# Eight chunks of the modulation matrix worked on by TensorE inside the first attention instead of by VectorE beside the output projection

## The reference

```
cond = silu(c)
mod = cond @ w_ada + b_ada            # 2048 x 12288: shift1, scale1, gate1, shift2, scale2, gate2
h = rms(x, norm1_w) * (1 + scale1) + shift1
u, q, k, v = split(h @ w_in)
y_ssm = s5_mixer(u);  y_ssm = y_ssm * sigmoid(y_ssm @ w_glu)
y_att = dilated_attention(q, k, v)    # 8 heads of 128
x = x + gate1 * (concat(y_ssm, y_att) @ w_out)
h2 = rms(x, norm2_w) * (1 + scale2) + shift2
x = x + gate2 * swiglu_ffn(h2)
```

## Time and profile before

| | |
|---|---|
| three runs | 3303.84, 3310.92 and 3312.99 us, median 3310.92 |
| the profiled execution | 3305.19 us; its span 3303.4 us |
| TensorE busy | 3132.1 us, 95% of the span |
| VectorE busy | 1927.0 us, 58% |
| ScalarE busy | 1210.0 us, 37% |
| DMA | 630.47 MB, mean 191 GB/s |
| first attention's units | from 424.8 to 473.6 us of the span |
| first matmul of `glu`, of `w_out` | 480.70 us, 506.81 us |
| last matmul of `w_out` | about 616.5 us |

### The profile page before, as it was taken

The page is one execution under the profiler, slowest core; times in us unless marked ns, Lnnn a source line. Parts: engine busy times, 40 slices in busy tenths (PEclk is TensorE's granted clock), DMA queues, the critical chain, the costliest instruction groups (busy, mean ns, idle before and its releaser), DMA issues.

```text
span 3303.4 us, 57521 instructions
## 1 busy us (share of the span) xinstructions
PE 3132.1 (95%) x25282; PEld 3072.8 (93%) x25282; DVE 1927.0 (58%) x1816; ACT 1210.0 (37%) x1058; POOL 201.6 (6%) x194
## 2 busy tenths in 40 slices
PE   3399978899999999999999999999999999999999
PEld 2399858799999999999999999999899999999999
DVE  7999768776444444745445544564556554555454
ACT  2254433333333333433333333343334333333333
POOL 3344130000000000000000000000030000000000
PEclk6699969899999999999999999999999999999999
DMA  9776608678555555555555555567635555555554
GB/s 336 250 260 241 237 31 289 217 259 283 179 183 190 183 186 190 181 176 170 175 178 171 173 178 178 169 190 135 124 127 179 182 188 186 184 190 180 189 183 136
DMA packets 328703, 630.47 MB, mean 191 GB/s; under 512 B 22453, under 2 KB 24009, under 8 KB 328281
## 3 DMA queue, kind: packets, MB, share of 16 engines
q1 hardware_dynamic: 317512, 624.79, 57.8%
q10 hardware_dynamic: 11040, 3.51, 0.5%
HBM read 626.16 MB, written 2.10 MB: 190 GB/s over the span
## 4 chain that ended last, share of the span: by engine, by line
PE 81%; DVE 3%; issue 1%; ACT 1%; DVEq 0%; ACTq 0%
PE ps L545 23%; PE ps L546 23%; PE ps L547 23%; PE ps L1861 2%; PE ps L1863 2%; PE ps L1862 2%; PE ps L1898 1%; PE ps L1899 1%; PE ps L1900 1%; DVE w_lo L412 1%; DVE accb L426 0%; ACT w_hi L407 0%; PE ps L1802 0%; PE ps L1776 0%; PE ps L1812 0%
## 5 line engine op out<-in xcount | busy, mean ns | idle before, releaser
L412 DVE TENSOR_TENSOR w_lo<-raw,w_hi 128x2048 fp32r<-128x2048 f32 x496 | 1141.0, 2301 | 1229.5 <-ACT w_hi L407 1229.3
L407 ACT ACTIVATE w_hi<-raw 128x2048 fp32r<-128x2048 f32 x496 | 949.8, 1915 | 1777.9 <-PE ps L547 1550.9
L545 PE MATMUL ps<-act_hi,w_hi 128*128 128x256 f32 (+1 forms) x4288 | 1221.9, 285 | 46.0 <-DVE w_lo L412 23.1
L546 PE MATMUL ps<-act_lo,w_hi 128*128 128x256 f32 (+1 forms) x4288 | 1219.0, 284 | 0.0
L547 PE MATMUL ps<-act_hi,w_lo 128*128 128x256 f32 (+1 forms) x4288 | 1217.3, 284 | 0.0
L545 PEld LDWEIGHTS ps<-act_hi,w_hi 128*128 128x128 f32 x4288 | 814.1, 190 | 49.4 <-issue 29.4
L545 PE MATMUL ps<-hid_hi,w_hi 128*128 128x256 f32 (+1 forms) x2880 | 814.4, 283 | 7.1 <-DVE w_lo L412 7.1
L546 PEld LDWEIGHTS ps<-act_lo,w_hi 128*128 128x128 f32 x4288 | 813.8, 190 | 0.0
L547 PEld LDWEIGHTS ps<-act_hi,w_lo 128*128 128x128 f32 x4288 | 813.4, 190 | 0.0
L547 PE MATMUL ps<-hid_hi,w_lo 128*128 128x256 f32 (+1 forms) x2880 | 812.4, 282 | 0.0
L546 PE MATMUL ps<-hid_lo,w_hi 128*128 128x256 f32 (+1 forms) x2816 | 794.5, 282 | 0.0
(11 more groups left out here) (328 smaller groups left out, 2050.1 us busy)
## 6 DMA issues: line engine op xcount, KB each, us to landing
raw<-in_w_ada SPq DMA_DIRECT2D x96, 1024.0 KB, 5.1
raw<-in_ffn_w_gate SPq DMA_DIRECT2D x88, 1024.0 KB, 5.0
raw<-in_ffn_w_up SPq DMA_DIRECT2D x88, 1024.0 KB, 5.0
raw<-in_ffn_w_down SPq DMA_DIRECT2D x88, 1024.0 KB, 5.1
raw<-in_w_in SPq DMA_DIRECT2D x64, 1024.0 KB, 6.3
raw<-in_w_ffn_gate SPq DMA_DIRECT2D x44, 1024.0 KB, 5.0
raw<-in_w_ffn_up SPq DMA_DIRECT2D x44, 1024.0 KB, 5.1
raw<-in_w_ffn_down SPq DMA_DIRECT2D x44, 1024.0 KB, 5.1
```

What stands on the lines that cost most here:

```text
L407: act.activation(w_hi[b][:, :, :], raw[j % RING][:, :, :], ACT.Copy).then_inc(hi_ready, 1)
L412: dve.tensor_tensor(w_lo[b][:, :, :], raw[j % RING][:, :, :], w_hi[b][:, :, :].bitcast(F32), ALU.subtract).then_inc(lo_ready, 1)
L545: pe.matmul(o, whi, hi[:, k, cols], start=(k == 0 and not (shared and m % 2)), stop=False)
L546: pe.matmul(o, whi, lo[:, k, cols], start=False, stop=False)
```

## The change

Eight of the 16 V chunks leave `w_out`, whose pass is now `VSS` four times (8 V and 16 S chunks in all). They form a new phase `mid` of kind `P` between `w_in` and `glu`. TensorE multiplies them itself, out of `raw`, without VectorE: for each of 4 row tiles and 4 column tiles one matmul with the weights as stationary operand and one column of `cond` as moving operand, accumulated in PSUM bank 5. `beside(s_)` of the attention now does half a chunk, eight matmuls, in each of the steps 0 to 15. VectorE adds the bias at the end of the block. The ring's head at the end of `w_in` is now four `mid` chunks; the other four and the head of `glu` are issued during the attention.

```diff
-    add("w_out", 2, 2, 4, "VS" * 8)
+    add("mid", 1, 0, 4, "P" * 8)
...
+    add("w_out", 2, 2, 4, "VSS" * 4)
...
+            if name == "mid":
+                return lambda it, j: w_ada(j % 4, SCALE2 * P + (j // 4) * GROUP)
...
-            return {"S": (lo_ready, n), "V": (acc_step, CK * n)}[p.order[j]]
+            return {"S": (lo_ready, n), "V": (acc_step, CK * n), "P": (mid_done, n)}[p.order[j]]
...
-                stream(sp, "glu", rest=False)
+                stream(sp, "mid", rest=False)
...
+        def mid_pe(pe, s_):
+            p = byname["mid"]
+            for e in range(MID // 8 * s_, MID // 8 * (s_ + 1)):
+                j, half = divmod(e, 2)
+                if j >= MID:
+                    continue
+                if half == 0:
+                    landed(pe, p, 0, j)
+                for t in (2 * half, 2 * half + 1):
+                    for m in range(4):
+                        c = 4 * (j // 4) + m
+                        mm = pe.matmul(ps[:, 5, c:c + 1], raw[j % RING][:, t, P * m:P * m + P], cond[:, CK * (j % 4) + t:CK * (j % 4) + t + 1],
+                                       start=(e == 0 and t == 0 and m == 0), stop=(j == MID - 1 and t == CK - 1 and m == 3), skip_group_check=True)
+                if half:
+                    mm.then_inc(mid_done, 1)
...
+                stream(sp, "mid", head=False)
+                stream(sp, "glu", rest=False)
...
                 units_dve(dve, 0)
+                dve.wait_ge(mid_done, MID)
+                dve.tensor_tensor(gain[:, 0:MID], ps[:, 5, 0:MID], bada[:, SCALE2:SCALE2 + MID], ALU.add)
...
-                units_pe(pe, 0, nothing)
+                units_pe(pe, 0, lambda s_: mid_pe(pe, s_))
...
-                    dve.wait_ge(mod_sum, 20)
-                    link(dve, "dve", dve.tensor_tensor(gain[:, :], ps[:, 1, 0:16], bada[:, SCALE2:SCALE2 + 16], ALU.add))
+                    dve.wait_ge(mod_sum, 18)
+                    link(dve, "dve", dve.tensor_tensor(gain[:, MID:16], ps[:, 1, 0:16 - MID], bada[:, SCALE2 + MID:SCALE2 + 16], ALU.add))
...
-                for g in range(4):
+                for g in range(2):
```

More of the change, by code:

```diff
@@ L28 @@
 QUADS = KT // 4
+MID = 8
 SEQ = 256
@@ L100, in __init__ @@
         self.body = len(order)
-        self.per = {k: order.count(k) for k in "SV"}
+        self.per = {k: order.count(k) for k in "SVP"}
         self.n0 = tally["n"]
-        self.before = {k: tally[k] for k in "SV"}
+        self.before = {k: tally[k] for k in "SVP"}
         self.g0 = tally["g"]
         tally["n"] += iters * self.body
-        for k in "SV":
+        for k in "SVP":
             tally[k] += iters * self.per[k]
@@ L119, in plan @@
 def plan():
-    tally = {"n": 0, "g": 0, "S": 0, "V": 0}
+    tally = {"n": 0, "g": 0, "S": 0, "V": 0, "P": 0}
     ph = []
@@ L312, in build @@
         wf_split, wf_in = sem("wf_split"), sem("wf_in")
+        mid_done = sem("mid_done")
         tile_done, tile_free = sem("tile_done"), sem("tile_free")
@@ L337, in source @@
                 w = rows(a[name][0], 0, D)
-                first = GATE1 if name == "w_in" else SCALE2
-                return lambda it, j, v=None: w_ada(v % 4, first * P + (it * 2 + v // 4) * GROUP) if v is not None else w[:, CK * (j % 4):CK * (j % 4) + CK, bass.ds((j // 4) * GROUP + it * (2 * GROUP), GROUP)]
+                first, per = (GATE1 * P, 2) if name == "w_in" else (SCALE2 * P + (MID // 4) * GROUP, 1)
+                return lambda it, j, v=None: w_ada(v % 4, first + (it * per + v // 4) * GROUP) if v is not None else w[:, CK * (j % 4):CK * (j % 4) + CK, bass.ds((j // 4) * GROUP + it * (2 * GROUP), GROUP)]
             ffn, what = name.split(".")
@@ L837, in gate2_dve @@
         def gate2_dve(dve):
-            dve.wait_ge(mod_sum, 24)
+            dve.wait_ge(mod_sum, 22)
             dve.tensor_tensor(mod[:, GATE2:GATE2 + 16], ps[:, 4, 0:16], bada[:, GATE2:GATE2 + 16], ALU.add).then_inc(mod_read, 1)
```

## The result

The changed kernel takes 3350.65 us (median of 4 runs, 3349.97 to 3351.61) against 3308.26 us before (4 runs). The ratio is 1.0134, with a 95% interval of 1.0122 to 1.0146: 42 us slower.

What follows compares the result with a forecast made beforehand. The prediction took TensorE, busy for 95% of the span, to bound the kernel. Its terms, 4.7 + 52.8 + 0.2 - 3.9 = +53.8 us on a base of 3308, gave 3361 us, with a range of 3320 to 3372.

Steps and rivals of the forecast that it cites:

- Which stage pays, and why: Attention: the added matmuls lengthen TensorE's queue, +4.7 and +52.8 us; loads and DMA issues add nothing.
- slow pairs: Attention, two steps (one head) at clock 0.50: 5.91 us before, TensorE the bound; 12.6 us forecast with the change.
- The clock: Attention: the granted clock stays at the lower level, 0.50, for the whole stage; likeliest case, chance 0.64.
- full-clock rival: Attention: the added work lifts TensorE to the full clock; +12.5 us, 3320 us; chance 0.10.
- Steps 0 and 1: Start of the attention: half chunks at the lower clock, the first partly hidden in a wait; +1.3 and +3.5, together +4.7 us.
- Steps 2 to 15: Attention: seven pairs of steps at 12.6 us each, 88.2 us against 35.4; +52.8 us, bounds +47.9 and +54.6.
- The start of `w_out`: Second split comes earlier, TensorE's stop shrinks from 2.52 to about 0.4 us, no clock fall follows; -3.9 us.
- The three group ends: Later groups of w_out: a V chunk still precedes the third split, so TensorE's 3.19 us stops remain; 0 us.
- steps 16 and 17: End of the attention, up to the last weighing: they add nothing.
- VectorE's addition: Block's end, on the path into glu: VectorE's small addition costs about 0.2 us.
- likeliest case: Whole kernel with the attention at the lower clock: 3361 us, own range 3351 to 3370; chance 0.64.
- Two of the signs: Profile of the changed kernel: attention ends some 57 us later in the span; new matmuls stand 0.217 us apart.

Runs made afterwards that it cites:

- run with one matmul of eight: The changed kernel with only one matmul of each eight in the attention, all loads, waits and the w_out order kept: 3302.74 us, ratio to before 0.9988.
- runs with 128 columns: The changed kernel with 128 equal moving columns instead of one in every mid matmul: 3311.29 us; with w_out order VSSSVS as well, 3298.54 us.
- exchanged operands: The changed kernel with the column of cond stationary and 512 weights moving in the mid matmuls: 3318.82 us, ratio to before 1.0036.
- 64-column run: The changed kernel with 64 equal moving columns instead of one in every mid matmul: 3351.38 us, ratio to before 1.0137.
- run with the other order: The changed kernel with w_out in the order VSSSVS instead of VSSVSS: 3342.23 us, ratio to before 1.0106.

## Why the prediction was right

*Which stage pays, and why.* Right. TensorE's own queue was the bound in the slow pairs, and the added matmuls stand in it one behind another. The run with one matmul of eight shows that next to nothing else of the move costs time (0.6 us in the stage): loads and waits are covered as the text said.

*The clock.* Right, and it was the largest choice: 0.50 throughout. The full-clock rival failed in its plainest form: 54.6 us of unbroken matmuls with one moving column stayed at 0.50. The evidence in the prediction was thin, one window of 2 us. The same trace has a stronger row, the two pairs of the kernel before in which TensorE shows no idle row:

```profile
446.00:457.80 11.80, 11.71 (x35) 8.44 (x34) 9.66 (x38) 3.65 (x12) 8.74 (x5) 0.50 0.00 0
```

The rule that the prediction names, of the Trainium skill, page "TensorE: Matmul & The Clock Gate", section "Why this matters for your kernels", is to keep TensorE continuously busy. These traces do not agree with it for matmuls with one or 64 moving columns (0.50), and agree with it for 128 (1.00). My own reason was that the single columns thin out what had at times brought the clock up. It fits the runs with 128 columns and with exchanged operands; from the 64-column run I had expected a rise by the same reason, and none came, so it is not shown as it stands.

*Steps 0 and 1.* +4.7 forecast. From the first spread (422.89) to that of step 2 (437.17) it is 14.3 us; before it was 10.3 (424.77 to 435.07): +4.0.

*Steps 2 to 15.* This is the mis-sized term: +52.8 forecast, +46.8 measured (437.17 to the end of step 15's half chunk at 519.38, 82.2 us, against 35.4). Two things are in it. A pair is 12.11 us, not 12.6, because its two half chunks cost 3.28 and 3.34 us and not 3.47 each, and because the old work shrinks from 5.91 to 5.49 when nothing in it waits. So the slow pair did hide some 0.4 us of waiting, although its window showed TensorE fully busy; I had weighed the upper bound too heavily, the lower one, 11.9, was nearer. And the seventh pair has no spread and only one of its two scores, since there is no ninth head: it takes 9.6 us. This is half of the 6.0 us. Counting seven equal pairs ignored the end of the loop, which was in the code.

*The start of `w_out`.* Right: the stop of 0.38 us against "about 0.4", and no fall behind it.

*The three group ends.* Right: 3.20, 3.19 and 3.21 us, at the same place of VectorE's order. The run with the other order shows the cause: VectorE's total load is the same there, and the stops are gone. One of the three falls of the clock did not come (1.00 in the window from 592 to 620), which makes -5.4 out of the forecast -3.9, near the end of its range. From stop to stop that group took 26.05 us (593.78 to 619.83), the next, with its fall, 27.50. The forecast that the clock would fall in every group was wrong for this one.

*The end.* The sum was +53.8 and the profiled executions differ by 44.8. Of the 9.0 us between them, 6.0 are the steps 2 to 15, 0.7 the steps 0 and 1, 1.5 `w_out`, above all the missing fall, and 0.2 the steps 16 and 17. The rest, 0.6, is the span ahead of the attention (1.9 shorter) less the stretches behind it that came out longer. VectorE's addition, put at 0.2 without a row, took 0.15 us. The medians differ by 42.4 us only, since the profiled execution of the kernel before lay 3.1 us under its median and that of the changed kernel 0.7. So 3361 (3308 and 53.8 would be 3362) was 10 us too high; 3350.65 lies inside the stated range of 3320 to 3372, and just under the 3351 at which the likeliest case alone was to end. The mechanism was right; the 10 us are above all the mis-sized term. Two of the signs came out otherwise: the stage ended 48.7 us later in the span (522.3 against 473.6), not 57, and the new matmuls stood a little closer than the gathers did, 0.209 us against 0.217.

What stays open: why the clock of the attention without added work had a mean of 0.64 in one execution and 0.57 in another; why it stayed down with 64 columns and came up with 128, for which no run lies between them or with another spacing; and why a 3.2 us stop brings a fall in some groups and not in others.

## What to carry to other kernels

Work moved onto an engine that looks idle must be priced at the clock that this work itself will get: here a matrix-vector product with one moving column held TensorE at the lower level and cost nearly twice its price at the other (0.209 against 0.113 us a record). Before giving such a form up, try to fill the moving side: here 128 equal columns added next to nothing to a record at the full clock and saved 39 us, while 64 saved nothing. And of an engine's in-order list, ask not how much is taken off but what still stands between the last result and the next wanted one; one chunk of each group moved by one place was worth 12 us in the stage, while eight chunks taken away elsewhere were worth 5.

## What the runs showed of the hardware that was not expected

- With float32 weights of 128 x 128, 64 moving columns raised the distance of the records at the clock 0.50 from 0.209 to about 0.216 us only: a half chunk took 3.45 us from its start to the next spread (460.95 to 464.40) against 3.34.
- At the clock 1.00 the distance with 128 columns was about 0.117 us (447.88 to 449.76, 16 records), and the gathers with one column had 0.113: the columns are nearly free there as well.
- 256 such records with one column kept TensorE and its weight loads busy for 54.6 us at a granted clock of 0.50. With 128 columns, and with 512 weights moving past one column of `cond`, the clock was 1.00 inside the attention.
- The attention without added work took 48.8 us at a mean clock of 0.64 in one profiled execution and 51.8 us at 0.57 in another.
- Three equal stops of 3.2 us in `w_out` were followed by a fall of the clock in all three groups of the kernel before (0.50 in the windows of 2 us from 550.4, 578 and 605.6) and in two of three of the changed kernel (0.50 from 619.8 and 647.3, 1.00 from 593.8).
